# Expert weights of a mixture-of-experts layer: six 2 MB pieces an item, or two pairs of 4 MB and two single pieces

## What is computed

```python
logits = xt @ w_router + b_router
top_val, top_idx = lax.top_k(logits, 4)          # of 32 experts
gates = softmax(top_val)
...
hh = xb @ w_gu[e] + b_gu[e]                      # 1024 -> 2048
glu = minimum(hh[:, :1024], 7.0)
lin = clip(hh[:, 1024:], -7.0, 7.0)
act = glu * sigmoid(1.702 * glu) * (lin + 1.0)
y = (act @ w_down[e] + b_down[e]) * gate         # 1024 -> 1024
out[token] += y
```

## Time and profile before

| | us |
|---|---|
| median of 3 runs | 1198.6 (1197.23 to 1200.29) |
| the profiled execution, own time | 1198.85 |
| its span, first to last instruction | 1197.1 |
| TensorE busy (matmul) | 1139.1, 95% of the span |
| VectorE, ScalarE busy | 282.5 and 170.9 |
| bytes read from HBM | 433.31 MB |
| chain that ended last: DMA, TensorE | 43% and 40% of the span |

### The profile page before, as it was taken

The page is one execution under the profiler, slowest core; times in us unless marked ns, Lnnn a source line. Parts: engine busy times, 40 slices in busy tenths (PEclk is TensorE's granted clock), DMA queues, the critical chain, the costliest instruction groups (busy, mean ns, idle before and its releaser), DMA issues.

```text
span 1197.1 us, 16918 instructions
## 1 busy us (share of the span) xinstructions
PE 1139.1 (95%) x7060; PEld 482.6 (40%) x7060; DVE 282.5 (24%) x576; ACT 170.9 (14%) x317; POOL 0.2 (0%) x4
## 2 busy tenths in 40 slices
PE   7999999999999999999999999999999999999997
PEld 6888866533333333333333333333333332333334
DVE  2455635321111111112112111111111111111123
ACT  3323422211000000000110000000000000000014
POOL 0000000000000000000000000000000000000000
PEclk9999999999999999999999999999999999999999
DMA  9732125579999999999999999999999999999970
GB/s 372 320 141 73 38 107 212 228 297 400 428 428 427 428 429 429 429 429 428 429 428 428 429 429 428 427 429 429 429 429 428 429 428 429 429 429 429 425 312 36
DMA packets 32228, 434.90 MB, mean 363 GB/s; under 512 B 3840, under 2 KB 4096, under 8 KB 5952
## 3 DMA queue, kind: packets, MB, share of 16 engines
q1 hardware_dynamic: 32192, 434.37, 86.4%
HBM read 433.31 MB, written 1.05 MB: 363 GB/s over the span
## 4 chain that ended last, share of the span: by engine, by line
DMA 43%; PE 40%; ACT 0%; DVE 0%; issue 0%; SPq 0%; DVEq 0%
DMA ring<-in_we 42%; PE PS L855 27%; PE PS L940 2%; PE PS L703 2%; PE PS L817 2%; PE PS L832 2%; PE PS L869 1%; PE PS L824 1%; PE PS L899 0%; PE PS L753 0%; DMA hT<-in_wproj 0%; PE PS L879 0%; PE PS L759 0%; PE PS L498 0%; PE PS L840 0%
## 5 line engine op out<-in xcount | busy, mean ns | idle before, releaser
L855 PE MATMUL PS<-ring,FV 128*64 128x512 f32 x2304 | 515.4, 596 | 25.5 <-DMA ring<-in_we 25.5
L855 PEld LDWEIGHTS PS<-ring,FV 128*64 128x64 f32 x2304 | 158.1, 137 | 364.0 <-issue 302.7
L855 PE MATMUL PS<-B,FV 128*64 128x512 f32 x768 | 174.0, 595 | 9.4 <-DMA B<-in_we 8.7
L855 PEld LDWEIGHTS PS<-B,FV 128*64 128x64 f32 x768 | 53.0, 137 | 114.4 <-issue 98.6
L486 PE MATMUL PS<-hT,ring 128*128 128x256 f32 x416 | 93.0, 382 | 0.8 <-ACT hT L993 0.6
L486 PEld LDWEIGHTS PS<-hT,ring 128*128 128x128 f32 x416 | 78.1, 190 | 12.2 <-ACT hT L993 0.8
L1474 DVE TENSOR_SCALAR rz<-con,lora 64x64 f32<-64x64 f32 x30 | 7.4, 247 | 306.1 <-PE PS L855 306.1
L1556 DVE TENSOR_SCALAR hT<-PS 128x512 f32<-128x512 f32 x32 | 22.1, 692 | 185.1 <-PE PS L855 185.1
L1247 DVE TENSOR_TENSOR FV<-PS,prm 128x512 f32<-128x512 f32 x32 | 22.1, 692 | 183.8 <-PE PS L824 183.8
L817 PE MATMUL PS<-xq,rz 128*64 128x512 f32 x256 | 62.0, 605 | 0.0
L1152 ACT ACTIVATE FV<-PS 128x512 f32<-128x512 f32 x32 | 19.1, 597 | 297.8 <-PE PS L899 297.8
(11 more groups left out here) (266 smaller groups left out, 675.3 us busy)
## 6 DMA issues: line engine op xcount, KB each, us to landing
ring<-in_we SPq DMA_DIRECT2D x144, 2048.0 KB, 23.9
B<-in_we SPq DMA_DIRECT2D x48, 2048.0 KB, 29.3
ring<-in_wz SPq DMA_DIRECT2D x7, 2048.0 KB, 22.8
ring<-in_wo SPq DMA_DIRECT2D x2, 2048.0 KB, 8.1
ring<-in_wgate SPq DMA_DIRECT2D x2, 2048.0 KB, 38.8
xq<-in_x SPq DMA_DIRECT2D x2, 512.0 KB, 5.3
ring<-in_wz SPq DMA_DIRECT2D x1, 1024.0 KB, 8.5
xq<-in_x SPq DMA_DIRECT2D x1, 1024.0 KB, 4.8
```

Of the source, the lines that this page charges most:

```text
L855: mm = pe.matmul(PS[64 * h:64 * h + 64, bank_, :], lhs(4 * (q % 2) + k), w[:, k, h, :], start=(first and k == 0), stop=(q % 2 == 1 and k = ...
```

## The change

On the host the expert weights are laid out in four arrays rather than one: pieces 0 and 1 joined so that a partition's row has 32 KB, piece 2, pieces 3 and 4 joined, piece 5. SP fetches a joined pair as one transfer of 4 MB, and the wait before it is that for the *second* product of the pair in its place (`LAST` = 1, 2, 4, 5). TensorE waits at product 0 and at product 3 for the whole pair, since a pair has one semaphore. `extra34` spans the first two extra places. Three things stay single: the six pieces of item 0, pieces 3 and 4 of the last item (`last_in_turn`), and all pieces 2 and 5. The order of the items in the second loop is turned round (odd, even), which is only how the last item comes out of the loop. The bytes are the same.

```diff
--- before.py
+++ after.py
@@ -210,6 +210,7 @@
         mixT = hT
         PP = B[:, 12:14, :]
         extra = [B[:, 4 * a:4 * a + 4, :].rearrange("p a n -> p (a n)") for a in range(NEXTRA)]
+        extra34 = B[:, 0:8, :].rearrange("p a n -> p (a n)")
         h2T = B[:, 12:14, :].rearrange("p a n -> p (a n)").rearrange("p (k t) -> p k t", k=KD)
         wgate = ring[:, 3:5, :]
         gfin = ring[:, 5, 0:D]
@@ -258,8 +259,10 @@
         s_bd = sem("b_down_landed")
         s_x2 = sem("x_again_landed")
         s_bt = sem("expert_bias_landed")
-        s_we = [sem(f"expert_piece{q}_landed") for q in range(6)]
-        s_odd = [sem(f"odd_expert_piece{q}_landed") for q in range(3, 6)]
+        s_up = [sem("expert_pieces01_landed"), sem("expert_piece2_landed")]
+        s_down = [sem("expert_pieces34_landed"), sem("expert_piece5_landed")]
+        s_odd = [sem("odd_expert_pieces34_landed"), sem("odd_expert_piece5_landed")]
+        s_last4 = sem("last_expert_piece4_landed")
         s_ple = sem("layer_projection_landed")
         s_ple1 = sem("layer_projection_second_half_landed")
         s_gate = [sem(f"gate_weights{q}_landed") for q in range(2)]
@@ -334,7 +337,9 @@
                     sp.dma_start(brt[:, :], t["brt"]).then_inc(s_aux, 16)
 
             def first_item(q):
-                sp.dma_start(ring[:, q, :], t["we"][0, q]).then_inc(s_we[q], 16)
+                src = t["we"][(0, 0, 1, 2, 2, 3)[q]][0]
+                half = slice(0, 4 * D) if q in (0, 2, 3, 5) else slice(4 * D, 8 * D)
+                sp.dma_start(ring[:, q, :], src[:, half]).then_inc((s_up if q < 3 else s_down)[int(q in (2, 5))], 16)
 
             def after(n):
                 sp.wait_ge(s_pe, pe_at[f"z{n}"])
@@ -360,8 +365,7 @@
             sp.dma_start(xq[:, :], t["x"]).then_inc(s_x2, 16)
 
             sp.wait_ge(s_pe, pe_at[f"y{NC - 1}"])
-            for a in range(2):
-                sp.dma_start(extra[a], t["we"][1, 3 + a]).then_inc(s_odd[a], 16)
+            sp.dma_start(extra34, t["we"][2][1]).then_inc(s_odd[0], 16)
             sp.wait_ge(s_dve, dve_at[f"o{NPAIR - 1}"])
             sp.dma_start(bT, t["bT"]).then_inc(s_bt, 16)
             sp.wait_ge(s_pe, pe_at["var"])
@@ -369,22 +373,26 @@
             sp.dma_start(pTt.rearrange("p k t -> p (k t)"), t["pT"]).then_inc(s_ple, 16)
 
             sp.wait_ge(s_dve, dve_at["mix"])
-            sp.dma_start(extra[2], t["we"][1, 5]).then_inc(s_odd[2], 16)
+            sp.dma_start(extra[2], t["we"][3][1]).then_inc(s_odd[1], 16)
             sp.wait_ge(s_pe, pe_at["xo10"])
             first_item(4)
             sp.wait_ge(s_pe, pe_at["xo11"])
             sp.dma_start(wproj0.rearrange("p k n -> p (k n)"), t["wproj"][0]).then_inc(s_ple, 16)
             first_item(5)
 
-            def place(q, odd):
-                return extra[q - 3] if odd and q >= 3 else ring[:, q, :]
-
-            def landed(q, odd):
-                return s_odd[q - 3] if odd and q >= 3 else s_we[q]
-
-            for q in range(6):
-                sp.wait_ge(s_used, q + 1)
-                sp.dma_start(place(q, q < 3), t["we"][1 if q < 3 else 2, q]).then_inc(landed(q, q < 3), 16)
+            def pieces(n):
+                return ring[:, n:n + 2, :].rearrange("p a n -> p (a n)")
+
+            PLACES = (pieces(0), ring[:, 2, :], pieces(3), ring[:, 5, :])
+            ODD_PLACES = (pieces(0), ring[:, 2, :], extra34, extra[2])
+            LAST = (1, 2, 4, 5)
+
+            def landed(m, odd):
+                return s_up[m] if m < 2 else (s_odd if odd else s_down)[m - 2]
+
+            for m in range(4):
+                sp.wait_ge(s_used, LAST[m] + 1)
+                sp.dma_start(PLACES[m], t["we"][m][1 if m < 2 else 2]).then_inc(landed(m, False), 16)
 
             sp.wait_ge(s_used, 7)
             for k in range(2):
@@ -397,32 +405,45 @@
             def weights(i, a=0):
                 return sp.value_load(EI[0:1, bass.ds(i + a, 1)], min_val=0, max_val=NE - 1)
 
-            def load(e, q, odd):
-                sp.dma_start(place(q, odd), t["we"][bass.ds(e, 1), q, :, :].rearrange("a p n -> (a p) n"))\
-                    .then_inc(landed(q, odd), 16)
+            def load(e, m, odd):
+                sp.dma_start((ODD_PLACES if odd else PLACES)[m], t["we"][m][bass.ds(e, 1), :, :].rearrange("a p n -> (a p) n"))\
+                    .then_inc(landed(m, odd), 16)
 
             def ahead(i, odd):
 
                 e, e_next = weights(i), weights(i, 1)
-                for q in range(6):
-                    sp.wait_ge(s_used, 6 * i + (q - 5))
-                    load(e if q < 3 else e_next, q, odd == (q < 3))
-
-            def in_turn(i, odd, qs=range(6)):
+                for m in range(4):
+                    sp.wait_ge(s_used, 6 * i + (LAST[m] - 5))
+                    load(e if m < 2 else e_next, m, odd == (m < 2))
+
+            def in_turn(i, odd, ms=range(4)):
 
                 e = weights(i)
-                for q in qs:
-                    sp.wait_ge(s_used, 6 * i + (q - 5 if q < 3 else q - 11))
-                    load(e, q, odd)
+                for m in ms:
+                    sp.wait_ge(s_used, 6 * i + (LAST[m] - 5 if m < 2 else LAST[m] - 11))
+                    load(e, m, odd)
+
+            def last_in_turn(i):
+
+                e = weights(i)
+                for m in range(2):
+                    sp.wait_ge(s_used, 6 * i + (LAST[m] - 5))
+                    load(e, m, True)
+                for a in range(2):
+                    sp.wait_ge(s_used, 6 * i + (a - 8))
+                    sp.dma_start(extra[a], t["we"][2][bass.ds(e, 1), :, 4 * D * a:4 * D * (a + 1)].rearrange("a p n -> (a p) n"))\
+                        .then_inc(s_odd[0] if a == 0 else s_last4, 16)
+                sp.wait_ge(s_used, 6 * i - 6)
+                load(e, 3, True)
 
             with sp.Fori(0, EARLY) as p:
                 ahead(2 * p + 2, False)
                 ahead(2 * p + 3, True)
-            in_turn(2 * EARLY + 2, False, range(3))
-            in_turn(2 * EARLY + 3, True)
+            in_turn(2 * EARLY + 2, False, range(2))
             with sp.Fori(EARLY, pairs) as p:
+                in_turn(2 * p + 3, True)
                 in_turn(2 * p + 4, False)
-                in_turn(2 * p + 5, True)
+            last_in_turn(2 * last_pair + 1)
             for q in range(2):
                 sp.wait_ge(s_used, 12 * last_pair + (q + 4))
                 sp.dma_start(wgate[:, q, :], t["wgate"][q]).then_inc(s_gate[q], 16)
@@ -841,15 +862,18 @@
                                        start=False, stop=False, skip_group_check=True)
                     finish(mm, "tpe", f"s{b}")
 
-            def product(i, odd, q, bank_, lhs, first):
+            def product(i, odd, q, bank_, lhs, first, last=False):
                 weights = extra[q - 3] if odd and q >= 3 else ring[:, q, :]
                 w = weights.rearrange("p (k h c) -> p k h c", k=4, h=2)
                 if q < 3:
-                    pe.wait_ge(s_we[q], 16 * i + 16)
+                    pe.wait_ge(s_up[q // 2], 16 * i + (32 if q < 2 else 16))
                 elif odd:
-                    pe.wait_ge(s_odd[q - 3], 8 * i + 8)
+                    if last and q == 4:
+                        pe.wait_ge(s_last4, 16)
+                    else:
+                        pe.wait_ge(s_odd[q // 5], 8 * i + 8)
                 else:
-                    pe.wait_ge(s_we[q], 8 * i + 16)
+                    pe.wait_ge(s_down[q // 5], 8 * i + (32 if q < 5 else 16))
                 for k in range(4):
                     for h in range(2):
                         mm = pe.matmul(PS[64 * h:64 * h + 64, bank_, :], lhs(4 * (q % 2) + k), w[:, k, h, :],
@@ -901,7 +925,7 @@
                 if not last:
                     gather(i + 2)
                 pe.wait_ge(s_aT, i + 1)
-                product(i, odd, 4, 4, act_of, True)
+                product(i, odd, 4, 4, act_of, True, last)
                 if not last:
                     turn(i + 2)
                 product(i, odd, 5, 4, act_of, False)
@@ -1709,7 +1733,10 @@
         host[f"wz{n}"] = chunks(w_in[:, c0:c0 + w])
     gu = a["w_gu"][0].reshape(NE, 2, 4, P, 2, FF).transpose(0, 4, 1, 3, 2, 5).reshape(NE, 4, P, 4 * FF)
     dn = a["w_down"][0].reshape(NE, 2, 4, P, D).transpose(0, 1, 3, 2, 4).reshape(NE, 2, P, 4 * D)
-    host["we"] = np.concatenate([gu, dn], 1)
+    host["we01"] = np.concatenate([gu[:, 0], gu[:, 1]], -1)
+    host["we2"] = gu[:, 2]
+    host["we34"] = np.concatenate([gu[:, 3], dn[:, 0]], -1)
+    host["we5"] = dn[:, 1]
     host["bT"] = np.concatenate([a["b_gu"][0][:, 0:FF], a["b_gu"][0][:, FF:]], 0)
     host["bdn"] = np.tile(a["b_down"][0], (P // NE, 1))
 
@@ -1719,6 +1746,7 @@
         w = np.ascontiguousarray(w)
         arrays[f"in_{name}"] = w
         t[name] = nc.dram_tensor(f"in_{name}", w.shape, mybir.dt.from_np(w.dtype), kind="ExternalInput").ap()
+    t["we"] = [t["we01"], t["we2"], t["we34"], t["we5"]]
```

## The result

Median 1208.95 us (7 runs, 1204.83 to 1209.87) against 1200.29 for the kernel before on the same chips: ratio 1.0068, interval 1.0055 to 1.0081. The change makes the kernel slower, by 8.7 us in the medians (6.6 to 9.7 by the interval of the ratio) and by 10.6 in the spans of the two profiled executions (1207.7 and 1197.1). The 1200.29 is a median of 7 runs of the kernel before; the 1198.6 that the prediction started from was the median of the first 3 of them.

A forecast was written before the change was run, and what follows sets the result against it. SP's DMA queue at 428 GB/s (29.37 us an item) was taken to set the end, with its dry moments and TensorE's remaining work; 2.0 + 5.2 + 4.2 - 1.0 = 10.4 us on 1198.6 gave 1209.0, range 1204.8 to 1213.0.

The forecast's parts named there:

- three losses: Time lost at item 0's start (+2.0 us), at item 10's change of fetching order (+5.2) and at the end (+4.2).
- Start: Items 0 to 2: later issue of joined pairs leaves the queue's landings 2 us later (1.5 to 2.7).
- Hole: Change of fetching order at item 10: item 11's pair goes into an empty queue, +5.2 us (4.5 to 5.5).
- Tail: Items 30 and 31: product 3 of item 30 waits for piece 4, so TensorE ends later, +4.2 us.
- Rate: Full queue: 32 KB rows were expected to change its speed little, -1 us (-4 to +2).
- Rival (a): Full queue over 28 items: fewer, longer rows or transfers speed it enough, 434.5 GB/s, to pay for the losses; 14%.
- Items 3 to 9 and 13 to 30: No time change; TensorE's waits gather into one of 2.2 us, before product 0, then before product 3.
- rival (c): TensorE's single 2.2 us waits make the clock fall, 1.5 us a fall; two falls an item give 1224; 4%.
- a rate over 430 in the long stretch: Sign of being wrong: the queue's GB/s exceeding 430 in the long stretch, where 428 was measured before.
- a granted clock below 1 between 300 and 1130 us: Sign of being wrong: the clock falling in the long stretch, where it was 1.00 before.
- The 1150 that I gave for a fixed price of each transfer: Whole kernel: at roughly 2 us per transfer, 61 merged would free over 100 us, ending near 1150; trace speaks against it.

The follow-up runs named there:

- the last version: Changed kernel with pieces 0 and 1 single in items 1, 8 to 12, 28 to 31, pieces 3 and 4 in 2, 3, 28 to 31; ratio 0.9998 to before.

## Why the prediction was right, and which terms were not

The median was forecast at 1209.0 and came at 1208.95. That it was hit so closely is luck: the sum was a change of 10.4 us on 1198.6, and measured was a change of 8.7 (6.6 to 9.7) on 1200.29, so the forecast change lies a little above its interval. The three losses and their mechanism were right. Step by step, from the two profiled executions:

- **Item 0 starts 1.5 us later** (243.29 for 241.75), which I had not counted. It doesn't seem to be the change's: in the profiles of the experiments the start lies between 239.1 and 243.2, at 239.1 to 239.8 in the three whose granted clock is 1.00 from 225 to 245 us, at 241.4 to 241.7 where it is 0.91 (before too) and from 242.0 up at 0.83, as here.
- **Start, forecast +2.0, measured +2.4.** Item 10's pair lands at 531.0, its piece 1 before at 528.1: +2.9, less 1.5, plus the 1.0 that the faster queue had won by then.
- **Hole, forecast +5.2, measured +6.5.** Piece 4 of item 30 landed at 1115.4 before and lands at 1122.0 with the pair: +6.6, less 2.9, plus 2.8 of rate. The sequence was as worked out, an empty queue and a transfer that landed 12.1 us after its issue (forecast 12.7, 0.6 too much). The rest is the fall of the clock at 531: products 0 and 1 took 8.8 us instead of 7.1, and nobody but the queue waited for them.
- **Tail, forecast +4.2, measured +4.1.** Product 3 of item 31 starts 10.7 us later than before, 6.6 of it the queue's.
- **Rate, forecast -1, measured -3.8.** This is the term that was mis-sized: 0.14 us in each of 27 items. I took the equal GB/s of 8 and 16 KB rows in short stretches as a sign that the length doesn't matter; the run with 8 KB rows shows 422 against 428. The value stood at the end of the range that I gave. Rival (a) had the mechanism right and its size at a third of what it needed.
- **Items 3 to 9 and 13 to 30, forecast nothing.** The waits came as single lumps, 2.05 us before product 0 from item 5 on (with one of 0.39 at item 4 already) and 1.9 us before product 3 from item 14, a little shorter than the 2.2 forecast; the queue's item was 0.15 us shorter. But rival (c) was partly real: the clock fell in four of those lumps, in none twice. Three of the falls were paid out of the next wait, as I had said of one fall an item, and the fourth stood at the hole.

1.5 + 2.4 + 6.5 + 4.1 - 3.8 = 10.7 us, and the spans differ by 10.6. So the total of this pair came out because the error in the rate (2.8) and the 1.5 and 1.7 us stand against each other. The medians differ by less than this pair of executions; without the 1.5 us the pair gives 9.1. The hole (4.3 us when mended) and the tail (3.6) are shown by runs of their own; the start has none, it was mended only together with the others.

Two of the signs that I had named for being wrong came true, a rate over 430 in the long stretch (431) and a granted clock below 1 between 300 and 1130 us (0.99). Both point at terms that were mis-sized, the rate and the clock, and neither at the three losses. The 1150 that I gave for a fixed price of each transfer was loose too: 2.2 us less in each of 28 items takes 1198.6 to 1137.

## What to carry over

Where a queue sets the end and runs full, joining transfers changed its rate here only as far as the rows got longer, by 0.5%; what it costs is found at the places where the queue is short of work, when it fills, when the order of fetching changes and at the end, and there a load that waits for two buffers rather than one leaves the queue empty. Count for each such place when the second buffer is free and how much the queue still holds, and join only where that is far more than the landing time. The engine that waits goes by a transfer's last landing, so a gain in GB/s need not reach it.

## What I had not expected of the hardware

- A row costs its DMA engine some 9 ns beside its bytes, at 8, 16 and 32 KB alike: 422, 428 and 431 GB/s (the last with a third of the bytes in rows of 16 KB). The number of transfers at the same row length made no difference (428 with 4 MB and with 2 MB). The Trainium skill (DMA: Bandwidth & Descriptors, section Why small descriptors are slow) has a fixed overhead of about 3 cycles a packet, and 32 bytes of descriptor beside it; the runs agree that there is an overhead, and find it larger, 9 ns being 8 cycles of the 850 MHz that the page gives.
- The same idle time of TensorE in one lump of 2 us rather than in 0.6 and 1.25 us lets the granted clock fall to 1.2 GHz now and then, 1.7 us a fall: four times between 300 and 1130 us in the trace of the changed kernel, in three of its four lumps of 2.05 us and in one of its sixteen of 1.9; ten times with rows of 16 KB, where the lump is 2.0 to 2.2 us; never in the trace of the kernel before. Most falls are free, as the next wait is shorter by as much.
- The 16 landings of one transfer are spread over 2.0 us in the kernel before and over 4.2 us at the end of the last version, and the waiting engine starts on the last of them.
